# A two-block transformer on one core: the second block's indexer moved ahead of retention, its softmax heads and gated linear attention moved with it, and the head norms computed from columns

## The chip, the cores and the metric

The kernel runs on one core of a Trainium2 chip. The metric is the device time of one execution in microseconds (us). TensorE is called PE here, VectorE DVE, ScalarE ACT, GpSimd POOL and SyncE SP.

## What is computed

All values are float32, the batch is one, the sequence has 512 tokens and the model 1024 columns. A first block of two layers (mLSTM, a Fourier branch, a convolution, an MLP) is untouched. The second block has two layers, each of this form (shortened from the reference; every line is 512 rows):

```
h   = rms_norm(x, pre_norm) * (1 + scale) + shift
p   = split(h @ w_in)                       # 7764 columns
ret = retention(rope(p.ret_q), rope(p.ret_k), p.ret_v)      # 4 heads, chunks of 128
ret = rms_norm(ret) * silu(p.ret_g)         # norm per head, over its 128 columns
# indexer: for each query a score of each visible key, the 128 best are kept
score = sum_h idx_w[h] * relu(rope(p.idx_q[h]) @ rope(p.idx_k).T / 8), causal
sel   = top_k(score, 128)
dsa = softmax(rope(p.dsa_q) @ rope(p.dsa_k).T / 8, keys in sel) @ p.dsa_v   # 8 heads, 2 kv heads
dsa = dsa * silu(p.dsa_g)
log_a = log_sigmoid(p.gla_a @ gla_w_lr + gla_b_lr) / 16
gl  = rms_norm(gla(p.gla_q, p.gla_k, p.gla_v, log_a)) * silu(p.gla_g)       # norm per head
g   = sigmoid(p.merge)                      # three gates of 1024 columns
y   = (g0 * (ret @ w_br_ret) + g1 * (dsa @ w_br_dsa) + g2 * (gl @ w_br_gla)) @ w_out
x   = x + gate * rms_norm(y, post_norm)
```

## The kernel before, in words

**Layout.** Activations stay in SBUF with the columns on the partitions and the tokens along the free dimension. Weights stream from HBM in slabs of 128 x 1024 values through a ring of six. A product against `w_in_2` is made exact enough by splitting: ACT copies a slab to the rounded form `WHI` (L2051), POOL subtracts it from the slab to give `RGR` (L2440), and PE runs three rounded matmuls for each of the eight row blocks (L985 to L987). A piece "F" is 128 output columns for all tokens, 24 matmuls. A piece "T" (L1007 to L1009) gives values with the tokens on the partitions. A piece "N" (L1028) multiplies the gated result of a branch by its output weights with four unsplit matmuls, each of which shows as two records.

**One order for all engines.** `schedule()` writes one list of steps. Each engine's program walks the same list and emits its part of each step, so the order in each engine's queue is the order of the list; an instruction that waits holds all behind it on its engine. Main work is written by `products()`. Side work is laid beside it: `begin(steps, period, credit)` opens a list, and after each part of a main piece `weave(us)` adds the part's planned microseconds to the list's credit and pops one step for each `period`. An F piece has three parts and 5.6 planned us, an N piece one part and 3.5, a T task 5.8. `end()` writes what is left of a list with nothing between. `products()` ends with `flush()`, which writes the pending second halves (`post`) of the last pieces.

**PSUM.** Main pieces of the second block take the banks 0 and 1 in turn; the first matmul of a piece waits until the last reader of its bank is done. A roped piece is copied out by ACT, and its `post` (one piece later) is a matmul with a permutation into bank 7 (L1148) and three DVE instructions (L1465, L1468, L1470); bank 7 is reused by the next.

**A second-block layer before** is, in order:
1. products ret_q, ret_k (roped), ret_v (T), ret_g, nothing beside them;
2. products idx_q, idx_k, the small columns `few`, dsa_q, dsa_k, dsa_v, dsa_g; beside them retention (`ret`, four chunks of three steps) and its norms (`rSq`, `rNorm`), period 3.5;
3. products gla_q, gla_k, gla_v (T), gla_g and branch 0 (eight F for the gates, eight N); beside them three lists: `top` (the indexer's products `idx`, L1324, L2357, L1879, and the selection `top`, L1891 and L1893, for the query blocks 1 to 3), period 2.2, and `head[0]`, `head[1]` (each 4 blocks x 4 heads x 3 steps), period 2.6;
4. branch 1; beside it `gated_stages` (the decays `gDecay`, `gStart`, eight levels of `gLevel`, `gOut`, `gState`, and the norms `gSq`, `gNorm`), period 2.4, 34 steps; what is left follows at once;
5. branch 2 and the product with w_out, nothing beside them.

**The selection.** Sixteen rounds per query block, each `max` (the 8 largest, L1891) and `match_replace` (L1893, which shows as a short load of the values and the replacement). Block b has 128(b+1) keys.

**A softmax head** (block b, head t of half q) is: PE logits into bank 3+q (L1338); DVE adds the mask (L1910), takes the maximum (L1912), negates it (L1914); ACT exponential with sum (L2365); DVE reciprocal (L1916) and scaling (L1918); PE transposes (L1343); a copy by DVE for q=0 (L1922) or ACT for q=1 (L2369); PE product with the values (L1350). DVE's part up to L1918 is one step, so DVE waits in it for ACT.

**A head norm** before: ACT squares (L2342, L2417), PE multiplies 128 x 512 squares by ones (L1313, L1414), ACT takes the root over 128 x 512 (L2348, L2423), DVE inverts 128 x 512 values (L1864, L2009), multiplies the head by them (L1866, L2011) and the silu gate by that (L1868, L2013).

**The decays** (`gDecay`, twice): PE L1360, four ACT instructions (L2376 to L2382) with table loads, DVE L1935 to L1941; then `gStart`: ACT L2386, DVE, ACT L2388, DVE, ACT L2393. The gate of a branch's F piece is a sigmoid on ACT (L2246), written right after the piece. A level of `gLevel` needs two DVE products of 128 x 1024 (L1969, L1970), after which PE (L1378) and the masked copies (L1983) go.

Of the kernel before, what the change touches and what calls it, by code (L numbers as in the profile page):

```python
# [9 lines left out]
ALU = mybir.AluOpType  # L10
# [13 lines left out]
ZD = 11264  # L24
# [37 lines left out]
def constants():  # L62
# [31 lines left out]
    put("causal", np.where(i[None, :] <= i[:, None], 0.0, NEG))  # L94
# [502 lines left out]
def second_layer(o, l):  # L597
# [6 lines left out]
    def T(c0, n, dst):  # L604
        return ("T", "w_in_2", l, 0, c0, n, "v2", None, {**g, "tiles": range(4), "dst": dst})
# [88 lines left out]
def design(nc, dram):  # L694
# [135 lines left out]
    GRS = [ar(ZD + 6144, 512), ar(ZD + 6656, 512)]  # L830
# [72 lines left out]
    def tensor(e):  # L903
# [404 lines left out]

        def rNorm(l, h):
            if h >= 2:  # L1310
                e.wait_ge(*at("retA", ("sqrt", l, h - 2)))
            e.wait_ge(*at("retA", ("square", l, h)))
            e.matmul(PB[2 + h % 2][:, :], ones, RSQ[h % 2], start=True, stop=True).then_inc(*up("retP", ("norm", l, h)))  # L1313

        def idx(l, b, h):
# [3 lines left out]
            if (b, h) == (1, 0):  # L1319
                e.wait_ge(*at("evacV", ("roped", o.last["roped", l, "evacA", "DIK"])))  # L1320
                e.wait_ge(*at("retV", ("norm", l, 3)))
            else:
                e.wait_ge(*at("topA", (l, b, h - 1) if h else (l, b - 1, 3)))
            e.matmul(PB[2][:, 0:nk], DIQ[r, t, b * 128:b * 128 + 128], DIK[r, 0, 0:nk], start=True, stop=True).then_inc(*up("topP", (l, b, h)))  # L1324

        def head(l, q, b, t, i):
# [18 lines left out]
            else:  # L1345
                e.wait_ge(*at((V, A)[q], (l, b, t, "PT")))
                if t == 0 and b:
                    e.wait_ge(*at(V, (l, b - 1, "gated")))
                for kt in range(b + 1):
# [59 lines left out]

        def gNorm(l, h):  # L1410
            if h >= 2:
                e.wait_ge(*at("glaA", ("sqrt", l, h - 2)))
            e.wait_ge(*at("glaA", ("square", l, h)))
            e.matmul(PB[2 + h % 2][:, :], ones, GSQ[h % 2], start=True, stop=True).then_inc(*up("glaP", ("norm", l, h)))  # L1414

        stages = {"mm": mm, "post": post, "xsum": xsum, "rstd": rstd, "residual": residual, "mPrep": mPrep, "mA": mA, "mB": mB, "mC": mC, "mD": mD, "mO": mO,
                  "ret": ret, "rNorm": rNorm, "idx": idx, "head": head, "gDecay": gDecay, "gLevel": gLevel, "gOut": gOut, "gState": gState,
                  "gNorm": gNorm}
# [4 lines left out]
    def vector(e):  # L1423
# [436 lines left out]

        def rNorm(l, h):
            rs, g = RRS[h % 2], G2["RETG"]
            e.wait_ge(*at("retA", ("sqrt", l, h)))
            e.reciprocal(rs, rs).then_inc(*up("retV"))  # L1864
            e.wait_ge(*now("retV"))
            e.tensor_tensor(RO[:, h, :, :], RO[:, h, :, :], v4(rs), MUL).then_inc(*up("retV"))  # L1866
            e.wait_ge(*now("retV"))
            e.tensor_tensor(v4(g[:, h, :]), v4(g[:, h, :]), RO[:, h, :, :], MUL).then_inc(*up("retV", ("norm", l, h)))  # L1868
# [13 lines left out]
        def top(l, b, i):  # L1882
            nk = 128 * (b + 1)
            sl = slice(b * 128, b * 128 + 128)
            if i == 0:
                e.wait_ge(*now("topV"))
                e.tensor_tensor(SC[:, sl], SC[:, sl], cst("causal"), ADD).then_inc(*up("topV"))
            for n in range(4 * i, 4 * i + 4):
# [685 lines left out]
```

## Time and profile before

| | us |
|---|---|
| median of 3 runs (lowest, highest) | 3643.05 (3642.25, 3647.4) |
| the profiled execution: its own time | 3641.63 |
| its span | 3639.8 |
| PE busy | 3236.4 (89%) |
| DVE busy | 1446.1 (40%) |
| ACT busy | 1064.6 (29%) |
| POOL busy | 966.5 (27%) |

The span runs from the first to the last instruction of the profiled execution; its own time is measured around it. PE's share of the whole says little on one stage: the stretches of the two layers of the second block begin at about 2066 us and 2873 us in the span, and are read one by one. The granted clock stands as a fraction of full speed: 1.00 is 2.4 GHz throughout, 0.50 is 1.2 GHz throughout.

### The profile page before, as it was taken

Reading aid. Unit: us, or ns where it says so; the run is one execution under the profiler, and the core shown is the slowest. Engines: PE = TensorE matmul, PEld = TensorE weight load, DVE = VectorE, ACT = ScalarE, POOL = GpSimd, SP = SyncE. Lnnn points to the kernel's source line nnn. Section 1 sums busy time; section 2 is a strip of 40 time slices with the busy share of each in tenths; the row PEclk is TensorE's granted clock in tenths of the full one; section 3 lists DMA queues with packets and bytes.
Section 4 is the critical chain, followed back from the end, with each engine's and each line's share of the span. In section 5 each row is a group of like instructions: output and inputs, shape, how many; then the busy total and the mean of one; then the engine's idle time right before and its main releaser. Section 6 shows DMA issues by size and latency. Waiting matters only on the chain.

```text
span 3639.8 us, 40425 instructions
## 1 busy us (share of the span) xinstructions
PE 3236.4 (89%) x16416; PEld 2511.0 (69%) x16416; DVE 1446.1 (40%) x2646; ACT 1064.6 (29%) x1668; POOL 966.5 (27%) x476
## 2 busy tenths in 40 slices
PE   6989789999999889689999899797899899797898
PEld 4678668888888668577777676554657776554656
DVE  1574433422332562435111425733531326732632
ACT  2213433321222312432323223243222223234222
POOL 0121113222224112133444233121125233111134
PEclk9999877999999799789999899899899799898899
DMA  5233331211111223213222212111012112111111
GB/s 189 96 119 111 131 135 47 70 64 61 62 64 64 77 93 128 87 58 108 93 93 93 70 65 66 38 47 52 29 54 91 64 65 67 38 47 46 35 63 65
DMA packets 78505, 277.29 MB, mean 76 GB/s; under 512 B 8416, under 2 KB 10080, under 8 KB 78192
## 3 DMA queue, kind: packets, MB, share of 16 engines
q1 hardware_dynamic: 74736, 267.86, 21.6%
q10 hardware_dynamic: 3584, 6.84, 0.5%
q8 instruction: 131, 2.15, 0.2%
q14 instruction: 54, 0.44, 0.0%
HBM read 272.57 MB, written 2.10 MB: 75 GB/s over the span
## 4 chain that ended last, share of the span: by engine, by line
PE 78%; DVE 13%; ACT 5%; issue 2%; DMA 1%; POOL 1%; ACTq 0%; DVEq 0%; SPq 0%; POOLq 0%
PE pb L985 17%; PE pb L987 16%; PE pb L986 16%; PE pb L1028 5%; PE pb L1096 3%; PE pb L1378 2%; PE pb L934 2%; PE pb L1007 1%; PE pb L1009 1%; PE pb L1008 1%; DVE AR L1893 1%; DVE AR L1891 1%; PE pb L1350 1%; PE pb L1338 1%; PE pb L1054 1%
## 5 line engine op out<-in xcount | busy, mean ns | idle before, releaser
L2440 POOL TENSOR_TENSOR RGR<-RG,WHI 128x1024 fp32r<-128x1024 f32 x330 | 794.0, 2407 | 2166.4 <-ACT WHI L2051 2166.4
L2051 ACT ACTIVATE WHI<-RG 128x1024 fp32r<-128x1024 f32 x330 | 345.1, 1046 | 368.2 <-PE pb L987 282.3
L985 PE MATMUL pb<-HI,WHI 128*128 128x512 f32 (+1 forms) x880 | 389.6, 443 | 24.2 <-POOL RGR L2440 11.1
L986 PE MATMUL pb<-HI,RGR 128*128 128x512 f32 (+1 forms) x880 | 357.9, 407 | 0.0
L987 PE MATMUL pb<-LO,WHI 128*128 128x512 f32 (+1 forms) x880 | 357.8, 407 | 0.0
L985 PE MATMUL pb<-HR,WHI 128*128 128x512 f32 (+1 forms) x768 | 278.8, 363 | 16.7 <-POOL RGR L2440 10.1
L987 PE MATMUL pb<-HR,WHI 128*128 128x512 f32 (+1 forms) x768 | 277.6, 361 | 0.0
L986 PE MATMUL pb<-HR,RGR 128*128 128x512 f32 (+1 forms) x768 | 277.3, 361 | 0.0
L987 PE MATMUL pb<-HIDR,WHI 128*128 128x512 f32 (+1 forms) x768 | 274.7, 358 | 0.0
L985 PE MATMUL pb<-HIDR,WHI 128*128 128x512 f32 (+1 forms) x768 | 273.7, 356 | 1.1 <-ACT RLT L2193 0.8
L986 PE MATMUL pb<-HIDR,RGR 128*128 128x512 f32 (+1 forms) x768 | 274.1, 357 | 0.0
L985 PEld LDWEIGHTS pb<-HI,WHI 128*128 128x128 f32 (+1 forms) x880 | 171.3, 195 | 96.6 <-issue 50.0
L1028 PE MATMUL pb<-AR,RG 128*128 128x512 f32 x384 | 193.9, 658 | 15.4 <-DVE AR L2013 15.4
L987 PEld LDWEIGHTS pb<-LO,WHI 128*128 128x128 f32 (+1 forms) x880 | 170.9, 194 | 44.7
L986 PEld LDWEIGHTS pb<-HI,RGR 128*128 128x128 f32 (+1 forms) x880 | 171.5, 195 | 43.0 <-issue 8.3
L1629 DVE TENSOR_TENSOR RLT<-RLT 128x256 f32<-128x256 f32 (+1 forms) x96 | 117.7, 1226 | 206.3 <-ACT RLT L2193 206.0
L985 PE MATMUL pb<-HH,WHI 128*128 128x512 f32 (+1 forms) x464 | 173.5, 374 | 23.6 <-POOL RGR L2440 10.5
L985 PEld LDWEIGHTS pb<-HR,WHI 128*128 128x128 f32 x768 | 146.8, 191 | 47.1 <-issue 24.2
L986 PE MATMUL pb<-HH,RGR 128*128 128x512 f32 (+1 forms) x464 | 166.6, 359 | 0.0
L987 PE MATMUL pb<-HL,WHI 128*128 128x512 f32 (+1 forms) x464 | 166.5, 359 | 0.0
L987 PEld LDWEIGHTS pb<-HR,WHI 128*128 128x128 f32 x768 | 146.8, 191 | 22.9
L986 PEld LDWEIGHTS pb<-HR,RGR 128*128 128x128 f32 x768 | 147.1, 192 | 22.5
(381 smaller groups left out, 5812.1 us busy)
## 6 DMA issues: line engine op xcount, KB each, us to landing
RG<-in_W_dram SPq DMA_DIRECT2D x504, 512.0 KB, 3.3
XCX<-in_xT_dram ACTq DMA_DIRECT2D x1, 2048.0 KB, 21.3
GRID<-in_grid_dram ACTq DMA_DIRECT2D x1, 2048.0 KB, 27.2
out_dram<-XCX SPq DMA_DIRECT2D x8, 256.0 KB, 2.0
CS<-in_CST_dram ACTq DMA_DIRECT2D x1, 1027.0 KB, 4.9
XCC<-in_ctxT_dram ACTq DMA_DIRECT2D x1, 1024.0 KB, 14.9
CS<-in_CST_dram SPq DMA_DIRECT2D x1, 523.0 KB, 4.6
RG<-in_W_dram SPq DMA_DIRECT2D x2, 256.0 KB, 2.9
```

Source lines behind the costliest of these rows:

```text
L934: i = e.matmul(PB[p["banks"][0]][32 * g:32 * g + 32, 0:256], CV[:, :, 4 * h + g], wt[:, g, :], start=h == 0, stop=h == 1, tile_position=(0 ...
L985: e.matmul(out, hi[:, k, :], xh, start=k == order[0], stop=False)
L986: e.matmul(out, lo[:, k, :], xh, start=False, stop=False)
L987: i = e.matmul(out, hi[:, k, :], xl, start=False, stop=k == order[7])
L1007: e.matmul(out, xh[:, sl], hi[:, k, :], start=h == 0 and i0 % per == 0 and k == 0, stop=False)
L1008: e.matmul(out, xh[:, sl], lo[:, k, :], start=False, stop=False)
L1028: i = e.matmul(out, wt[:, k, p["j"]:p["j"] + 128], G2[p["x"]][:, k, :], start=k == 0, stop=k == 3)
L1096: m = e.matmul(sum_at(tag, c), squares_at(tag, i)[:, a:a + 128], ones[:, 0:1], start=k == 0 and c == first, stop=k == 7 and c == 5)
L1378: m = e.matmul(PB[2 + bk][:, a:a + 128], ks[r, t, sl], qs[r, t, sl], start=True, stop=True)
L1629: e.tensor_tensor(r, r, r, MUL).then_inc(*up("evacV", ("hidden", i)))
L2051: e.activation(WHI[:, u % 2, 0:n], RG[:, s % RING, 0:n], ACT.Copy).then_inc(*up("weightsA", u))
L2440: e.tensor_tensor(RGR[:, s % RING, 0:n], RG[:, s % RING, 0:n], WHI[:, u % 2, 0:n].bitcast(F32), SUB).then_inc(*up("weightsG", u))
```

## The change

- **Order.** A layer begins with idx_q, idx_k and `few`. Then ret_q, ret_k, ret_v, ret_g with `top` beside them, period 3.0; `top` goes on beside dsa_q, dsa_k, dsa_v, dsa_g, where retention and its norms are also laid, period 2.5. Selection steps now hold two rounds instead of four (24 steps instead of 12).
- **Heads.** The two lists of heads, period 2.5, lie beside gla_q, gla_k, gla_v, gla_g and the first six jobs of branch 0 (three quarters of it). Beside the last quarter lie `gDecay`, `gDecay`, `gStart` (period 4.0, credit 4.0), and the rest of `gated_stages` lies beside branch 1 (period 2.0, credit -4.0, 33 steps).
- **Norms.** The gate is multiplied by the unnormed head at once. The squares are summed by PE against one column of ones, four matmuls per head, into 16 columns of bank 3; ACT takes one root and DVE one reciprocal of 128 x 16; PE spreads the factors, four 128 x 128 matmuls per head into banks 2 to 5; DVE multiplies the gate by them from PSUM.
- **Signs.** The mask is subtracted the other way round and the minimum taken, so that the negation (L1914) goes.
- **Banks.** The T tasks of ret_v write banks 2, 3 and then 0, 1; those of gla_v banks 0, 1 and then 2, 7. The indexer's products go to bank 6 instead of 2. Some tiles move in SBUF.

```diff
 def norm_stages(x, l):
-    out = []
-    for h in range(4):
-        out += [(x + "Sq", l, h)]
-        if h:
-            out += [(x + "Norm", l, h - 1)]
-    return out + [(x + "Norm", l, 3)]
+    return [(x + "Sq", l, h) for h in range(5)] + [(x + "Root", l)] + [(x + "Norm", l, h) for h in range(4)]
...
-    jobs = [F(C_RQ, 256, "roped", "evacA", dst="RQ"), F(C_RK, 256, "roped", "evacA", dst="RK"), T(C_RV, 512, "RVT"),
-                F(C_RG, 512, "silu", "evacA", dst="RETG")]
+    jobs = [F(C_IQ, 256, "roped", "evacA", dst="DIQ"), F(((C_IK, 64), (C_IK, 64)), 128, "roped", "evacA", dst="DIK"),
+            F(((C_GA, 16), (C_IW, 4)), 20, "few", "evacA")]
...
     o.products(jobs, (0, 1), 2)
-    ret = o.begin([("ret", l, c, i) for c in range(4) for i in range(3)] + norm_stages("r", l), 3.5)
-    o.products([F(C_IQ, 256, "roped", "evacA", dst="DIQ"), F(((C_IK, 64), (C_IK, 64)), 128, "roped", "evacA", dst="DIK"),
-                F(((C_GA, 16), (C_IW, 4)), 20, "few", "evacA"), F(C_DQ, 512, "roped", "evacA", dst="DQ"),
+    top = []
+    for b in (1, 2, 3):
+        top += [("idx", l, b, h) for h in range(4)] + [("top", l, b, i) for i in range(8)]
+    top = o.begin(top, 3.0)
+    o.products([F(C_RQ, 256, "roped", "evacA", dst="RQ"), F(C_RK, 256, "roped", "evacA", dst="RK"), T(C_RV, 512, "RVT", ((2, 3), (0, 1))),
+                F(C_RG, 512, "silu", "evacA", dst="RETG")])
+    ret = o.begin([("ret", l, c, i) for c in range(4) for i in range(3)] + norm_stages("r", l), 2.5)
+    o.products([F(C_DQ, 512, "roped", "evacA", dst="DQ"),
                 F(((C_DK, 64), (C_DK, 64), (C_DK + 64, 64), (C_DK + 64, 64)), 256, "roped", "evacA", dst="DK"),
                 F(C_DV, 128, "vheads", "evacA"), F(C_DG, 512, "silu", "evacA", dst="DSAG")])
     o.end(ret)
-    top = []
-    for b in (1, 2, 3):
-        top += [("idx", l, b, h) for h in range(4)] + [("top", l, b, i) for i in range(4)]
-    head = [[("head", l, q, b, t, i) for b in range(4) for t in range(4) for i in range(3)] for q in range(2)]
-    sides = [o.begin(top, 2.2), o.begin(head[0], 2.6, 1.3), o.begin(head[1], 2.6)]
-    o.products([F(C_GQ, 256, "gq", "evacA"), F(C_GK, 256, "cp", None, dst="GK"), T(C_GV, 512, "GVT"), F(C_GG, 512, "silu", "evacA", dst="GLAG")])
+    o.end(top)
+    heads = [o.begin([("head", l, q, b, t, i) for b in range(4) for t in range(4) for i in range(3)], 2.5, 1.25 * q) for q in range(2)]
+    o.on_bank[2] = ("retV", ("norm", l, 3))
+    o.on_bank[7] = ("evacA", ("turned", o.last["vheads", l, "evacA", None]))
+    o.products([F(C_GQ, 256, "gq", "evacA"), F(C_GK, 256, "cp", None, dst="GK"), T(C_GV, 512, "GVT", ((0, 1), (2, 7))),
+                F(C_GG, 512, "silu", "evacA", dst="GLAG")])
+    gated = gated_stages(l)
...
+        if br == 0:
+            o.products(jobs[0:6])
+            o.end(*heads)
+            start = o.begin(gated[0:3], 4.0, 4.0)
+            o.products(jobs[6:8])
+            o.end(start)
+            gated = o.begin(gated[3:], 2.0, -4.0)
+            continue
         o.products(jobs)
-        if br == 0:
-            o.end(*sides)
-            sides = [o.begin(gated_stages(l), 2.4)]
         if br == 1:
-            o.end(*sides)
+            o.end(gated)
...
+        def head_sums(h, squares):
+            for c in range(4):
+                m = e.matmul(PB[3][:, 384 + 4 * h + c:385 + 4 * h + c], squares[:, c * 128:c * 128 + 128], ones[:, 0:1], start=h == 0 and c == 0,
+                             stop=h == 3 and c == 3)
+            return m
+        def head_factors(h, roots):
+            for c in range(4):
+                m = e.matmul(PB[2 + h][:, c * 128:c * 128 + 128], roots[:, 4 * h + c:4 * h + c + 1].to_broadcast([128, 128]), ident, start=c == 0,
+                             stop=c == 3)
+            return m
...
-            e.reciprocal(rs, rs).then_inc(*up("retV"))
-            e.tensor_tensor(RO[:, h, :, :], RO[:, h, :, :], v4(rs), MUL).then_inc(*up("retV"))
-            e.tensor_tensor(v4(g[:, h, :]), v4(g[:, h, :]), RO[:, h, :, :], MUL).then_inc(*up("retV", ("norm", l, h)))
+            g = G2["RETG"][:, h, :]
+            e.tensor_tensor(g, g, PB[2 + h][:, :], MUL).then_inc(*up("retV", ("norm", l, h)))
...
-                e.tensor_tensor(L, PB[3 + q][:, 0:nk], MAS[b][:, 0:nk], ADD).then_inc(*up(V))
+                e.tensor_tensor(L, MAS[b][:, 0:nk], PB[3 + q][:, 0:nk], SUB).then_inc(*up(V))
-                e.tensor_reduce(mx, L, AX, MAX).then_inc(*up(V))
-                e.tensor_scalar(mx, mx, -1.0, None, MUL).then_inc(*up(V, (l, b, t, "max")))
+                e.tensor_reduce(mx, L, AX, MIN).then_inc(*up(V, (l, b, t, "max")))
```

## Rows read from the trace of the kernel before

**Rows 1.** The page's fourth part: the chain that ended last, by engine

```profile
PE 78%; DVE 13%; ACT 5%; issue 2%; DMA 1%; POOL 1%; ACTq 0%; DVEq 0%; SPq 0%; POOLq 0%
```

**Rows 2.** Stretches of layer one: length, PE, PEld, DVE, ACT, POOL busy; clock, DMA

```profile
2103.00:2246.00 143.00, 138.62 (x617) 101.84 (x617) 54.88 (x64) 43.31 (x60) 45.81 (x20) 1.00 0.21 68
2246.00:2319.00 73.00, 52.50 (x245) 36.69 (x243) 49.27 (x154) 18.04 (x43) 14.15 (x6) 0.84 0.15 49
2319.00:2380.00 61.00, 49.19 (x228) 35.35 (x228) 43.98 (x103) 19.00 (x33) 11.87 (x5) 0.85 0.11 35
2380.00:2520.00 140.00, 125.96 (x490) 76.39 (x490) 45.44 (x101) 50.45 (x75) 23.64 (x10) 0.96 0.15 49
2520.00:2645.00 125.00, 98.55 (x438) 70.64 (x437) 66.02 (x81) 39.28 (x41) 19.90 (x9) 0.84 0.10 34
2645.00:2708.00 63.00, 54.14 (x223) 35.25 (x222) 27.65 (x29) 19.48 (x30) 17.42 (x9) 0.95 0.18 59
```

**Rows 3.** Waits of PE in 2246:2520: total us, times, longest

```profile
PE pb L1343 <- DVE AR L1918: 29.1, 13, 6.9
PE pb L1007 <- DVE AR L1647: 14.8, 1, 14.8
```

**Rows 4.** Waits of PE in 2520:2720

```profile
PE pb L1378 <- ACT AR L2393: 15.9, 1, 15.9
PE pb L1378 <- DVE AR L1970: 10.6, 6, 3.1
PE pb L1028 <- DVE AR L2013: 7.7, 1, 7.7
```

**Rows 5.** DVE by line in 2246:2380: busy, mean ns, idle before

```profile
L1891 DVE MAX8 AR<-AR 128x8 f32<-128x256 f32 (+2 forms) x48 | 26.9, 561 | 1.5
L1893 DVE MATCH_REPLACE8 AR<-AR 128x256 f32<-128x256 f32 (+2 forms) x48 | 26.0, 542 | 0.0
L1879 DVE SCALAR_TENSOR_TENSOR AR<-AR 128x256 f32<-128x256 f32 (+2 forms) x9 | 8.2, 908 | 16.2 <-ACT AR L2357 16.1
```

**Rows 6.** DVE by line and shape in 2110:2720

```profile
L1864 DVE RECIPROCAL AR<-AR 128x512 f32<-128x512 f32 x4 | 13.4, 3351 | 9.1 <-ACT AR L2348 9.1
...
L1891 DVE MAX8 AR<-AR 128x8 f32<-128x512 f32 x16 | 11.1, 694 | 0.5
L1893 DVE MATCH_REPLACE8 AR<-AR 128x512 f32<-128x512 f32 x16 | 10.8, 676 | 0.0
...
L1465 DVE TENSOR_TENSOR AR<-AR,TAB 128x512 f32<-128x512 f32 x9 | 8.3, 927 | 0.0
...
L1866 DVE TENSOR_TENSOR AR<-AR 128x512 f32<-128x512 f32 x4 | 5.8, 1451 | 0.1
...
L1868 DVE TENSOR_TENSOR AR<-AR 128x512 f32<-128x512 f32 x4 | 4.8, 1210 | 0.1
```

**Rows 7.** ACT in order of time around the decays: start, us, what, idle before

```profile
2525.37 0.69 ACT L2376 ACTIVATE AR<-pb,VC 128x512 f32<-128x512 f32 x1 [10.58 <-PE pb L1360]
...
2538.24 0.60 ACT L2246 ACTIVATE AR<-pb 128x512 f32<-128x512 f32 x1
...
2550.84 0.60 ACT L2246 ACTIVATE AR<-pb 128x512 f32<-128x512 f32 x1
```

**Rows 8.** PE: a wait in ret_v; then the first and last matmul of an F piece

```profile
2089.82 0.36 PE L1007 MATMUL pb<-WHI,HI 128*128 128x256 f32 x1 [2.20 <-DVE AR L1647]
...
2527.91 0.50 PE L985 MATMUL pb<-HI,WHI 128*128 128x512 f32 x1
...
2533.39 0.40 PE L987 MATMUL pb<-LO,WHI 128*128 128x512 f32 x1
```

**Rows 9.** PE: sums against a column of ones, and spread factors, four matmuls each

```profile
2815.74 0.95 PE L1130 MATMUL pb<-CS,AR 128*128 128x1 f32 x8
...
2820.08 2.07 PE L1104 MATMUL pb<-CS,RSS 128*128 128x128 f32 x8 [1.64 <-DVE RSS L1496]
```

**Rows 10.** PE by shape in 2090:2820: retention's 16 matmuls of 128 columns

```profile
L1294 PE MATMUL pb<-AR 128*128 128x128 f32 x32 | 6.6, 303 | 0.0
```

More of the change, by code:

```diff
@@ L1307, in ret, with rSq @@
                 m.then_inc(*up("retP", (l, c, "KV")))
+        def head_sums(h, squares):
[8 more added lines that the diff above has]
+            return m
+        def rSq(l, h):
+            if h:
+                e.wait_ge(*at("retA", ("square", l, h - 1)))
+                head_sums(h - 1, RSQ[(h - 1) % 2]).then_inc(*up("retP", ("sums", l, h - 1)))
         def rNorm(l, h):
[L1310 to L1313, printed above, removed]
+            e.wait_ge(*at("retV", ("root", l)))
+            head_factors(h, RRS).then_inc(*up("retP", ("norm", l, h)))
         def idx(l, b, h):
@@ L1348, in head @@
                     e.wait_ge(*at(V, (l, b - 1, "gated")))
+                elif t == 0 and q:
+                    e.wait_ge(*at("topA", (l, 3, 3)))
                 for kt in range(b + 1):
@@ L1408, in gState, with gSq @@
             m.then_inc(*up("glaP", (l, c, "KV")))
+        def gSq(l, h):
+            if h:
+                e.wait_ge(*at("glaA", ("square", l, h - 1)))
+                head_sums(h - 1, GSQ[(h - 1) % 2]).then_inc(*up("glaP", ("sums", l, h - 1)))
         def gNorm(l, h):
[L1411 to L1414, printed above, removed]
+            e.wait_ge(*at("glaV", ("root", l)))
+            head_factors(h, GRS).then_inc(*up("glaP", ("norm", l, h)))
         stages = {"mm": mm, "post": post, "xsum": xsum, "rstd": rstd, "residual": residual, "mPrep": mPrep, "mA": mA, "mB": mB, "mC": mC, "mD": mD, "mO": mO,
-                  "ret": ret, "rNorm": rNorm, "idx": idx, "head": head, "gDecay": gDecay, "gLevel": gLevel, "gOut": gOut, "gState": gState,
-                  "gNorm": gNorm}
+                  "ret": ret, "rSq": rSq, "rNorm": rNorm, "idx": idx, "head": head, "gDecay": gDecay, "gLevel": gLevel, "gOut": gOut, "gState": gState,
+                  "gSq": gSq, "gNorm": gNorm}
         for what in o.steps:
@@ L1859, in ret, with rSq, rRoot @@
                               PB[4][:, 0:256].rearrange("p (t i) -> p t i", t=2)).then_inc(*up("retV", (l, c, "out")))
-        def rNorm(l, h):
-            rs, g = RRS[h % 2], G2["RETG"]
-            e.wait_ge(*at("retA", ("sqrt", l, h)))
-            e.reciprocal(rs, rs).then_inc(*up("retV"))
-            e.wait_ge(*now("retV"))
-            e.tensor_tensor(RO[:, h, :, :], RO[:, h, :, :], v4(rs), MUL).then_inc(*up("retV"))
-            e.wait_ge(*now("retV"))
-            e.tensor_tensor(v4(g[:, h, :]), v4(g[:, h, :]), RO[:, h, :, :], MUL).then_inc(*up("retV", ("norm", l, h)))
+        def rSq(l, h):
+            if h < 4:
+                g = v4(G2["RETG"][:, h, :])
+                if h == 0:
+                    e.wait_ge(*at("evacA", o.last["silu", l, "evacA", "RETG"]))
+                    e.wait_ge(*at("retA", (l, 3, "out")))
+                    e.wait_ge(*at("retV", (l, 3, "out")))
+                e.tensor_tensor(g, g, RO[:, h, :, :], MUL).then_inc(*up("retV", ("gated", l, h)))
+        def rRoot(l):
+            e.wait_ge(*at("retA", ("root", l)))
+            e.reciprocal(RRS, RRS).then_inc(*up("retV", ("root", l)))
+        def rNorm(l, h):
+            g = G2["RETG"][:, h, :]
+            e.wait_ge(*at("retV", ("gated", l, h)))
+            e.wait_ge(*at("retP", ("norm", l, h)))
+            e.tensor_tensor(g, g, PB[2 + h][:, :], MUL).then_inc(*up("retV", ("norm", l, h)))
         def idx(l, b, h):
@@ L1886, in top @@
                 e.wait_ge(*now("topV"))
-                e.tensor_tensor(SC[:, sl], SC[:, sl], cst("causal"), ADD).then_inc(*up("topV"))
-            for n in range(4 * i, 4 * i + 4):
+                e.tensor_tensor(SC[:, sl], SC[:, sl], cst("causal"), SUB).then_inc(*up("topV"))
+            for n in range(2 * i, 2 * i + 2):
                 src = SC if n == 0 else WK
@@ L2352, in idx @@
             e.wait_ge(*at("topP", (l, b, h)))
-            if (b, h) == (1, 0):
-                e.wait_ge(*at("retV", ("norm", l, 3)))
-            else:
+            if (b, h) != (1, 0):
                 e.wait_ge(*at("topV", (l, b, h - 1, "sum") if h else (l, b - 1, 3, "sum")))
-            e.activation(RLU[:, 0:nk], PB[2][:, 0:nk], ACT.Relu).then_inc(*up("topA", (l, b, h)))
+            e.activation(RLU[:, 0:nk], PB[6][:, 0:nk], ACT.Relu).then_inc(*up("topA", (l, b, h)))
         def head(l, q, b, t, i):
```

84 lines of the change are left out of this document (46 added, 38 removed).

## The prediction, made blind

> **What bounds the kernel now.** I read the chain first, then PE's waits, then stretches, then DVE and ACT inside them. The chain gives PE 78% and DVE 13% [rows 1]: the end is set by PE, which at some places waits for DVE. Those places are in the second block. In layer one PE is idle 4.4 us of 143 while retention runs (length less busy), 20.5 + 11.8 = 32.3 us of 134 where selection and the first heads run, 14.0 of 140 in the later heads, 26.5 of 125 in the decays and levels, 8.9 of 63 in the GLA outputs and norms: 86.1 us [rows 2]. Layer two repeats this within a few us, so every term counts twice.
>
> The reader is to see two more things in these rows. Where PE hardly waits the granted clock is 1.00; where it waits much it is 0.84 or 0.85, and in the late heads, whose 14 us of waits are short ones, still 0.96 [rows 2]. And DVE is busy 93 of 134 us in the first heads but only 45 of 140 after them: the difference is the selection, 26.9 + 26.0 + 8.2 = 61.1 us [rows 5]. DVE takes its steps in order, so heads and PSUM evacuations stand behind rounds of selection. One piece of gla_v waited 14.8 us for its bank that way [rows 3].
>
> **The change part by part**, for one layer, in us of PE's time (minus is gain).
>
> *Selection leaves the heads.* The first heads keep only their own chain, as the late ones have it. The 14.8 us of gla_v go, as DVE has no backlog and each T pair now has banks of its own. Of 32.3 us I leave 2, since blocks 0 and 1 have short rows: -30. Bounds: if the early heads waited at the late heads' rate, 14.0 / 140 x 134 = 13 stay (-19); at best all goes (-32).
>
> *Late heads.* Same products, same N pieces of 3.5 planned us that let two head steps meet without main work between; the negation goes, and the period falls from 2.6 to 2.5, which takes back about as much: -1, bounds -5 to +3.
>
> *Selection goes to retention's side.* 36 steps of 3.0 planned us are 108, over 67.9 + 61.6 = 129.5 planned us: all fit. Beside ret_q to ret_g DVE has little else. The tight place is block 3: its eight selection steps fall 19 to 40 us into the second group of products. DVE must do 16 x (0.694 + 0.676) = 22 us and the loads between [rows 6], four roped posts at 3 x 0.93 = 11 at most [rows 6], and about 9 of retention and gates: 42. PE has 21 of main work and some 13 of retention and ropes beside it: 34. Each retention step and each rope waits for DVE's step before it, so PE can't run ahead: 8 us of wait, 2 more for steps that meet a two-round step of 2.7 us: +10. Bounds: 3 (the excess absorbed by the light steps behind) and 48 (rival C). The same region had 4.4 us of waits, mostly behind the norm's root and DVE's 3.35 us reciprocals; of these I take 3.4 away. Net +6.6.
>
> *The first products.* ret_v's wait of 2.2 us for its bank [rows 8] goes, with the banks split. But the new first group ends with `few`, and the flush behind it makes PE wait for its copy (0.6, as the 0.60 of a bank [rows 7]) and for DVE's rope of idx_k (2 x 0.93 [rows 6]), with no piece between: +2.3. Together 0, bounds -2 to +2.
>
> *Norms by columns.* DVE loses 13.4 + 5.8 + 4.8 = 24.0 us per norm [rows 6] and gets four products into the gate (1.21 each), four from PSUM and one tiny reciprocal: about 8. At the end of GLA the reciprocals were what PE waited for: 7.7 [rows 4]. The new norm ends inside branch 1 and two F pieces pass before its reader: of 8.9 us [rows 2], -7.7. PE pays: 16 sums per norm. Four take 0.95 at full clock [rows 9]: 4.0. And 16 spreads, between 2.07 / 4 / 2 = 0.26 (that row ran at half clock) [rows 9] and 6.6 / 16 = 0.41 [rows 10], together 4.2 to 6.6, against four ones-products of about 0.87, 3.5, that go. So +4.7 to +7.1 per norm; I take 6, and +12 for two.
>
> The Trainium skill ("SBUF — State Buffer", section "Who interferes with whom") says that a DVE instruction with two SBUF inputs and a GpSimd instruction that reads SBUF exclude each other for their whole length. This case fits: L1866 and L1868 have two SBUF inputs and average 1.45 and 1.21 us [rows 6], over a one-input instruction's 0.69. It speaks for the multiplication from PSUM, and against laying 12 index sums, which have two SBUF inputs, beside products whose slabs POOL splits all the time; their 0.91 average [rows 5] has that in it only in part.
>
> *Decays beside branch 0.* This is where I differ most from what the order suggests. The wait of 15.9 us [rows 4] is the time of a serial chain ACT - DVE - ACT. From its first ACT instruction at 2525.37, the sigmoid of the F piece then in work leaves its bank at 2538.84 (+13.5), and that of the next one at 2551.44 (+26.1), because both stand behind decay steps in ACT's queue [rows 7]. The new order has the same shape: `gDecay` after the first part of the seventh job, `gDecay` at its end, ahead of that piece's sigmoid, `gStart` inside the next piece, ahead of its sigmoid. With a piece of 5.5 to 5.7 us [rows 8], PE starts the quarter at 0, the chain begins at 3.3, both F pieces are done at 13.3. The N piece behind needs the bank of the first: free at 16.8, a wait of 3.5. It takes 3.6; the second N needs the other bank: free at 29.4, a wait of 9.0. So 12.5 instead of 15.9: -3.4. Bounds: 0 if the sigmoids come through (-15.9), and 16.
>
> *Levels.* Per level PE offers 4 x 1.03 of its own and two steps' worth of main work, which falls from 4.8 to 4.0; DVE's two products, powers and masked copies don't change. The six waits of together 10.6 [rows 4] grow by about 0.4 each: +2.5, bounds 0 to +6. No steps are left over at branch 1's end any more (33 x 2.0 + 4 = 70 of 72.8 planned).
>
> *Clock.* (1 - clock) x length is 20.8 us in the early heads, 5.6 in the late, 20.0 in the decays and levels, 3.2 in the norms [rows 2]. Work loses this only while PE is busy, 0.76, 0.90, 0.79 and 0.86 of it: 15.8 + 5.0 + 15.8 + 2.8 = 39. The early heads give most back (-13), the norm its part and what the first pieces behind it lost (-4); the new waits beside retention take 4. So -13, bounds 0 to -25.
>
> The Trainium skill ("TensorE: Matmul & The Clock Gate", section "HAM oscillation — how this bites in real kernels") has PE fall back to the slow clock after idle gaps and prices throttled time at one half of it, as I do. The trace agrees only for the long waits: ten short ones left 0.96. If each new wait threw the clock back as the page's oscillating kernel shows, the 13 us would be none.
>
> Sum for a layer: -30 - 1 + 6.6 + 0 - 7.7 + 12 - 3.4 + 2.5 - 13 = -34.0; twice, -68. The profiled execution (3641.63, span 3639.8 and 1.8 around it) lies 1.4 under the median of 3643.05; from it the sum gives 3573.6, from the median 3575. I predict **3574**.
>
> **Rivals.**
>
> A, *the heads' waits are the price of their own chain*: early heads keep 13 us rather than 2, and the clock gives back nothing. For it: L1343's 29.1 us in 13 waits [rows 3], of which 14.0 us remain once selection is over [rows 2]. Against: blocks 0 and 1 have a quarter and a half of the last block's keys. Per layer -34 + 11 + 13 = -10: 3623. The clock rule of the page leads here too, by its half (-34 + 13 = -21: 3601).
>
> B, *the stalls go almost wholly*: the decays' sigmoids come through and leave 2 us (10.5 less), retention meets 4 (6 less), the norm costs 9 (3 less), the clock returns 25 (12 more). Per layer -34 - 31.5 = -65.5: 3512. For it: 1.00 in the stretch with retention now, though dense; against: the queue order above.
>
> C, *slower: DVE becomes the bound beside retention*. Twelve retention steps and four ropes each wait for a full selection step, 2 x 1.37 + 0.3 = 3.0: 48 us instead of 10, and the 60 us of main products beside them run at half clock, up to +30. Per layer -34 + 38 + 30 = +34: 3711. It decides from 34 us more wait and slow clock than I count. Against: rounds of blocks 1 and 2 are shorter, and DVE idles 88 of 143 us in that stretch now [rows 2].
>
> D, *no change*: the waits are the same ones under other names: new ones beside retention and in branch 0's end, and 12 us of added PE work, equal what goes; 3643. For it only the decays' part, which does so.
>
> **How the numbers follow.** Forecast 0.50, A 0.15, B 0.22, C 0.08, D 0.05. The range runs from 3505, just past B, to 3630, past A, and leaves C, D and a little of B's tail out. The likeliest case's own bounds: the terms at their near ends, some 17 us a layer either way, 3540 to 3608. About 0.2% (7 us) is what a measurement can tell from no change. Faster by more than that: forecast, A, B, less a little: 0.86. Within: D, 0.05. Slower: C and what is unforeseen, 0.09.
>
> **What would show it.** In the trace after: no wait of L1007 on DVE above 1 us; the early heads at clock near 1.00; waits of retention's lines or L1148 on the selection (L1891 to L1893) of 5 to 15 us a layer; a wait of an N piece (L1028) for ACT's sigmoid near the end of branch 0 of about 9 us; L1378's waits on DVE of 10 to 15; no wait on the last norm; DVE busy about 70 us less in all (16 per norm, 5 per layer for the negations). Wrong would be: more than 20 us of waits beside retention (C), more than 10 in the early heads (A), or under 4 at branch 0's end (B).

## The result and the profile after

The changed kernel took 3577.48 us in the median (3576.69 to 3578.79, four runs) against 3642.65 for the kernel before (3642.07 to 3647.4) on the same chip: ratio 0.9819, 95% interval 0.9802 to 0.9836. The forecast was 3574.0. The profiled execution has a span of 3574.9 us, 64.9 less than before.

From the first rope product of the second block's layer one to that of layer two it is 808.7 before and 773.4 after (-35.3), from there to the end 771.4 and 739.9 (-31.5), and the first block is 1.9 longer: -64.9.

From the page after, busy time by engine and then the chain that ended last, by engine:

```profile
PE 3236.3 (91%) x16640; PEld 2526.4 (71%) x16640; DVE 1374.9 (38%) x2570; ACT 1060.7 (30%) x1660; POOL 962.5 (27%) x476
...
PE 81%; DVE 10%; ACT 5%; issue 2%; DMA 1%; POOL 1%; ACTq 0%; DVEq 0%; SPq 0%; POOLq 0%
```

DVE went from 13% to 10% of the chain [rows 1] and has 71 us less work in all (forecast: about 70). Next, layer one of the second block in stretches, with columns as in [rows 2]. They are: indexer and first products; retention; early heads; late heads; decays; levels; GLA outputs and norm; the rest up to the next layer's first products.

```profile
2068.00:2165.00 97.00, 92.85 (x462) 69.83 (x464) 50.83 (x120) 23.83 (x34) 33.46 (x14) 0.97 0.21 71
2165.00:2271.00 106.00, 99.86 (x459) 73.87 (x457) 62.61 (x112) 26.62 (x39) 24.67 (x11) 0.94 0.16 53
2271.00:2361.00 90.00, 84.42 (x457) 64.23 (x457) 28.34 (x79) 30.67 (x62) 25.90 (x11) 0.98 0.19 62
2361.00:2487.00 126.00, 106.72 (x427) 65.92 (x425) 40.44 (x82) 47.66 (x71) 18.84 (x8) 0.92 0.14 46
2487.00:2519.00 32.00, 21.77 (x58) 11.84 (x57) 10.81 (x19) 20.40 (x22) 4.69 (x2) 0.84 0.10 33
2519.00:2609.00 90.00, 79.75 (x394) 59.18 (x393) 51.65 (x63) 21.50 (x21) 14.60 (x8) 0.91 0.13 41
2609.00:2665.00 56.00, 54.76 (x267) 38.80 (x266) 13.24 (x24) 19.96 (x28) 14.83 (x8) 1.00 0.14 47
...
2665.00:2842.00 177.00, 164.25 (x667) 123.09 (x665) 40.83 (x58) 47.02 (x67) 76.40 (x45) 0.90 0.24 81
```

To balance a whole layer, two stretches of the kernel before are needed that [rows 2] leaves out, ahead of and behind its six:

```profile
2066.00:2103.00 37.00, 33.76 (x220) 30.78 (x220) 7.72 (x10) 5.28 (x7) 10.74 (x5) 0.89 0.18 58
2708.00:2876.00 168.00, 154.71 (x613) 114.22 (x612) 40.08 (x58) 44.65 (x63) 72.21 (x42) 0.88 0.23 79
```

A stretch's first number less PE's busy time is PE's idle time. Over the layer it was 86.1 + 3.2 + 13.3 = 102.6 us before (810 us long) and is 69.6 after (774 us long): 33.0 less. The busy time fell by 3.0, from 707.4 to 704.4. So the layer's gain of 36 is nearly all waits. The 3.0 is what the clock gave back, less the work that the norms added. Layer two says the same: of its 31.4 us, 30.8 are idle time (107.1 to 76.3) and 0.6 busy time.

Waits of PE after, in the stretches 2165:2271, 2271:2361, 2361:2487 and 2487:2780, one fence (columns as in [rows 3]):

```profile
PE pb L1319 <- ACT AR L2391: 3.3, 1, 3.3
PE pb L1301 <- DVE AR L1867: 1.6, 1, 1.6
PE pb L1291 <- DVE AR L1886: 1.2, 1, 1.2
...
PE pb L1366 <- DVE AR L1954: 5.0, 5, 2.6
...
PE pb L1366 <- DVE AR L1954: 16.2, 9, 4.4
...
PE pb L1403 <- DVE AR L2006: 10.2, 6, 3.1
PE pb L1035 <- ACT AR L2293: 10.2, 2, 7.2
PE pb L1419 <- DVE AR L2039: 1.2, 1, 1.2
```

L1366 is the heads' transposes (L1343 before [rows 3]), L1403 the levels (L1378 [rows 4]), L1035 the N pieces (L1028), L1319 the new sums, L1291 and L1301 retention. The 14.8 of gla_v [rows 3], the 15.9 of the decays and the 7.7 of the last norm [rows 4] are gone. New are 10.2 at N pieces and 3.3 at the sums. Of the heads' waits before, 17.1 in 6 fell in 2246:2380 and 12.0 in 7 behind it.

### The profile page after: what moved, and what is told of

Its sections match the earlier page's. It is cut to its first block, busy times and chain, and to the rows that moved or that the text cites. A ratio compares the mean times of both kernels' runs of the same rounds, so it can differ in the third digit from the quotient of the medians.

```text
span 3574.9 us, 40795 instructions
## 1 busy us (share of the span) xinstructions
PE 3236.3 (91%) x16640; PEld 2526.4 (71%) x16640; DVE 1374.9 (38%) x2570; ACT 1060.7 (30%) x1660; POOL 962.5 (27%) x476
## 4 chain that ended last, share of the span: by engine, by line
PE 81%; DVE 10%; ACT 5%; issue 2%; DMA 1%; POOL 1%; ACTq 0%; DVEq 0%; SPq 0%; POOLq 0%
PE pb L992 18%; PE pb L994 17%; PE pb L993 17%; PE pb L1035 4%; PE pb L1103 3%; PE pb L1403 2%; PE pb L941 2%; PE pb L1014 2%; PE pb L1015 1%; PE pb L1016 1%; PE pb L1375 1%; PE pb L1061 1%; PE pb L1361 1%; PE pb L1111 1%; DVE AR L1624 1%
## 5 line engine op out<-in xcount | busy, mean ns | idle before, releaser
L1035 PE MATMUL pb<-AR,RG 128*128 128x512 f32 x384 | 189.7, 644 | 20.6 <-ACT AR L2293 20.6
```

Of the source, the lines that this page charges most:

```text
L1035: i = e.matmul(out, wt[:, k, p["j"]:p["j"] + 128], G2[p["x"]][:, k, :], start=k == 0, stop=k == 3)
```

## Experiments

A layer's length below is the 808.7 or 773.4 of above, taken the same way in the profiled execution of each kernel. In the versions of the changed kernel PE has the same instructions, so where a layer's busy time differs, they ran at another pace, in the main at another granted clock; only the idle time is waits. Both layers of every version, in us:

| kernel | layer one: length, idle, busy | layer two: length, idle, busy |
|---|---|---|
| before | 808.7, 101.6, 707.1 | 771.4, 107.1, 664.3 |
| before, norms alone | 797.7, 90.8, 706.9 | 765.0, 95.2, 669.8 |
| before, selection cut | 776.6, 78.5, 698.1 | 740.1, 84.7, 655.4 |
| changed | 773.4, 69.0, 704.4 | 739.9, 76.3, 663.7 |
| changed, again | 773.4, 69.0, 704.5 | 739.9, 76.3, 663.7 |
| changed, selection cut | 759.9, 62.9, 696.9 | 730.8, 68.9, 661.9 |
| `gStart` later | 764.7, 65.6, 699.1 | 735.1, 71.3, 663.9 |
| second `gDecay` later too | 776.6, 65.9, 710.7 | 737.8, 72.3, 665.5 |
| N pieces in halves | 776.0, 66.1, 709.9 | 739.2, 73.5, 665.7 |
| `gStart` later and halves | 767.8, 63.5, 704.3 | 734.9, 69.1, 665.8 |
| heads half a cycle apart | 759.0, 55.2, 703.9 | 728.3, 60.9, 667.5 |
| heads apart, `gStart` later | 759.6, 51.5, 708.1 | 724.2, 57.8, 666.4 |
| selection's period 2.6 | 776.9, 68.6, 708.3 | 744.4, 76.6, 667.8 |

**Norms alone.** The kernel before with only the new norms: `norm_stages`, sums, root and factors as in the change, order and heads untouched.

```diff
-    out = []
-    for h in range(4):
-        out += [(x + "Sq", l, h)]
-        if h:
-            out += [(x + "Norm", l, h - 1)]
-    return out + [(x + "Norm", l, 3)]
+    return [(x + "Sq", l, h) for h in range(5)] + [(x + "Root", l)] + [(x + "Norm", l, h) for h in range(4)]
```

> The kernel before with the column norms alone (order, banks, signs of before). Theory: DVE loses 16 us a norm; of PE's waits about 3.4 + 5 us beside retention and the first heads go, and the 7.7 us before branch 2; the clock gives 4 back; PE pays 8.6 us a layer (the 8.5 us of sums, 8.3 of spreads against 8.2 of ones-products read in the changed kernel). About -11 us a layer: 3620. Rival: the added PE work is all that shows, since other waits take the freed DVE time: +17, 3660. Second rival: the norms carry most of the change: 3590 or less.

Measured 3627.98 us (ratio to the kernel before 0.9951, 95% interval 0.9935 to 0.9968; the other runs are given in the same way); the layer is 797.7, 11.0 shorter. Its waits in the heads and decays:

```profile
PE pb L1355 <- DVE AR L1943: 28.5, 13, 6.9
PE pb L1002 <- DVE AR L1662: 14.8, 1, 14.8
...
PE pb L1390 <- ACT AR L2428: 15.9, 1, 15.9
PE pb L1390 <- DVE AR L1995: 10.5, 6, 3.0
```

They are those of [rows 3, 4] but for the 7.7 of the last norm, which is missing. Also gone are 3.4 us of waits for POOL's split (5.6 to 2.2 in the layer), which stood behind the old norm beside retention. The 5 us that the expectation took from the first heads did not go. With 8.6 us of work added, the layer's busy time stayed (707.1, 706.9), so its clock gave that much back; in layer two it gave back only 3.1. By length, the norms account for 11 of 35 us in layer one and 6.4 of 31.4 in layer two, and what is left, some 24 and 25, goes with the order, signs and banks. That split holds if the two add; the order alone was not run.

**Selection cut short, in the kernel before and in the changed one.** 4 of each block's 16 rounds are kept, 12 left out.

```diff
-            for n in range(4 * i, 4 * i + 4):
+            for n in range(i, i + 1):
```

> The kernel before with 4 of the 16 selection rounds in each query block (the other 12 are left out, so more keys stay masked out than should). Theory (DVE's backlog of selection is what the early heads wait for): the 14.8 us of gla_v and most of the 26.5 us of head waits before 2380 go, early heads keep about 5 us, clock there above 0.95; about -37 us a layer: 3570. Rival A (the heads' own chain is the price): 13 us or more of waits stay there beside a clock near 0.88; about -20 a layer: 3603.

```diff
-            for n in range(2 * i, 2 * i + 2):
+            for n in range(i // 2, i // 2 + 1 - i % 2):
```

> The changed kernel with 4 of the 16 selection rounds of each block kept and 12 left out (the same cut as in the kernel before, which there gave 3580.7 us, 62 to 65 us less). It tells how much the selection still costs in the new order. Theory (in the new order VectorE does the rounds beside products that don't wait for it): only the 5 to 8 us per layer of waits beside retention go, with 1 to 3 of clock, 3577 - 16 = about 3561 us. Rival (the selection still slows the layer through VectorE's queue and the shared memory everywhere): 30 to 45 us go, 3532 to 3547 us.

Measured 3580.7 (0.9825, 0.981 to 0.984) and 3555.7 (0.976, 0.9745 to 0.9774). In the kernel before the cut takes 62 to 65 us, in the changed one 22; by layer one 32.1 (to 776.6) and 13.5 (to 759.9). First the waits that the kernel before keeps with the cut, then those of the changed one, in the heads:

```profile
PE pb L1343 <- DVE AR L1918: 16.0, 12, 3.4
PE pb L1007 <- DVE AR L1647: 4.8, 1, 4.8
```

```profile
PE pb L1366 <- DVE AR L1954: 21.2, 14, 4.4
```

In the old place the selection cost 13.1 us of the heads' 29.1 and 10.0 of gla_v's 14.8. All of the 13.1 lie in the early heads (17.1 to 4.0); the late ones keep their 12.0. In the new place the heads' waits are the same with and without the rounds (5.0 + 16.2 above, 21.2 here), so nothing of them is selection. What the rounds still cost stands beside retention: with the cut the view of PE's waits lists none there, and the 6.1 us above are gone; the other 7.5 us of layer one (1.8 in layer two) are busy time, so clock. That is the move of the selection shown from both sides. The kernel before without the rounds is about as fast as the changed kernel with them.

**The decays' steps against the sigmoids.** Two orders of the same steps beside the last quarter of branch 0. `rest` is a step that does nothing.

```diff
-            start = o.begin(gated[0:3], 4.0, 4.0)
+            start = o.begin(gated[0:2] + [("rest",)] + gated[2:3], 4.0, 4.0)
```

> The changed kernel with gStart one part later, after the second sigmoid of branch 0's last quarter in ACT's queue. Theory (PE's wait of 7.2 us is for a sigmoid that stands behind gStart's three exponentials): that wait goes, the first of 3.0 stays, the levels start in time; -7 us of wait and -2 of slow clock a layer: 3560. Rival: the serial chain is the bound, and the same us come back as a wait of the first level: 3575 to 3578.

Measured 3563.85 (0.9777, 0.9763 to 0.9792), 13.6 us under the changed kernel. Its layers are 8.7 and 4.8 shorter; of these, 3.4 and 5.0 are waits, and 5.3 us of layer one are busy time. ACT in order of time, in the changed kernel (start, duration, instruction, idle before):

```profile
2500.40 0.60 ACT L2293 ACTIVATE AR<-pb 128x512 f32<-128x512 f32 x1
...
2503.25 1.06 ACT L2431 ACTIVATE AR<-AR 128x1024 f32<-128x1024 f32 x1
2506.96 1.06 ACT L2433 ACTIVATE AR<-AR 128x1024 f32<-128x1024 f32 x1 [2.65 <-DVE AR L1994]
2510.64 1.06 ACT L2438 ACTIVATE AR<-AR 128x1024 f32<-128x1024 f32 x1 [2.62 <-DVE AR L1985]
...
2513.01 0.60 ACT L2293 ACTIVATE AR<-pb 128x512 f32<-128x512 f32 x1
```

and in this one:

```profile
2500.62 0.60 ACT L2293 ACTIVATE AR<-pb 128x512 f32<-128x512 f32 x1
...
2502.06 0.59 ACT L2293 ACTIVATE AR<-pb 128x512 f32<-128x512 f32 x1
```

The second sigmoid (L2293) stood behind three exponentials (L2431 to L2438) and two waits for DVE, and comes 11 us sooner when it stands ahead of them. The N pieces' waits fall from 10.2 to the first one's 3.0. A new one of 3.5 appears, a bank that DVE's gateY holds, as gateY now stands behind DVE's part of `gStart`. So the N pieces' wait is a matter of place in ACT's queue, as the prediction had it. The total lands near the 3560 expected partly by luck: net waits fell by 8 us over both layers, not 14, and layer one's clock gave 5 more that its waits don't explain.

```diff
-            start = o.begin(gated[0:3], 4.0, 4.0)
+            start = o.begin([gated[0], ("rest",), gated[1], gated[2]], 4.0, 4.0)
```

> The changed kernel with the second gDecay after the first sigmoid and gStart after the second. Theory: both N pieces' waits (3.0 and 7.2 us a layer) shrink to under 2, one more table load each way on ACT; -8 us of wait and -3 of clock a layer: 3556. Rival: the chain is stretched by the sigmoids and ends about 5 us too late for the first level: 3565. Second rival (chain is the bound anyway): 3577.

Measured 3581.53 (0.9826, 0.9812 to 0.9841): a miss of 25 us. The waits for the sigmoids fell nearly as expected, from 10.2 to 2.2, but one of 4.8 for a bank that gateY holds (L1689) came in, which neither the theory nor its rivals had:

```profile
PE pb L992 <- DVE AR L1689: 4.8, 1, 4.8
PE pb L1035 <- ACT AR L2293: 2.2, 1, 2.2
```

7.0 against the changed kernel's 10.2, yet layer one is 3.2 longer. The layer in the changed kernel, with `gStart` later, and here (columns as in [rows 2]):

```profile
2061.54:2834.95 773.41, 704.38 (x3179) 506.75 (x3178) 298.16 (x556) 237.66 (x343) 213.25 (x104) 0.93 0.18 59
2061.67:2826.38 764.71, 699.10 (x3180) 504.09 (x3179) 298.62 (x556) 237.65 (x343) 213.27 (x104) 0.94 0.18 60
2069.28:2845.87 776.59, 710.69 (x3179) 511.31 (x3178) 297.88 (x556) 239.03 (x344) 213.26 (x104) 0.92 0.18 59
```

The idle time is 3.1 less here and the busy time of the same instructions 6.3 more, at a lower clock. Part of it lies behind the levels: in a stretch of 62 us PE was busy 60.76 us in both, but at a granted clock of 1.00 in the changed kernel and 0.94 here, about 3.6 us. Layer two, with the same edit, is 2.1 shorter, and the second block starts 7.7 later though nothing ahead of it differs. So this run tells little of the edit, and why its clock was lower is open.

**The changed kernel again, unaltered.**

> The changed kernel unaltered, on the same chip as the two others, to have its profile a second time: how far do two executions of the same instructions stand apart, and where. Expected: 3577 to 3580 us, each layer of the second block within 2 us of 774 us; the rival, that a kernel's lengths move by 5 us or more from load to load, would put the differences of the small experiments in doubt.

Measured 3581.68 (0.9828, 0.9813 to 0.9843), 4.2 us above the first time (the kernel before, run beside it, was 1.9 above its first time). Both layers are as long as the first time, and its second block starts at 2066.0 instead of 2061.5: all of the difference in span (3579.4 against 3574.9) arose in the first block. The four executions of this kernel lie between 3578.26 and 3585.01, and those of each of the two kernels with the heads moved, below, stand 9 us apart. So a difference in the total that is smaller than that says little of an edit; the idle time of the layer edited says more, and its length does where the busy time is the same.

**Heads: two guesses at the late waits.** First, N pieces handed out in halves with steps between:

```diff
-        return {"ada": 1.5, "N": 3.5, "G": 2.0}.get(p["kind"], 1.0)
+        return {"ada": 1.5, "N": 1.75, "G": 2.0}.get(p["kind"], 1.0)
...
-                    self.run(p, [(0, 1, 2, 3)], 3.5)
+                    self.run(p, [(0, 1), (2, 3)], 3.5)
```

> The changed kernel with one edit: the eight matmuls of an N piece are emitted as two parts of four with a step of each side queue between them, so that the two heads' steps no longer come back to back after 3.5 us of branch product. In the changed kernel the heads' transposes wait 19.3 us per layer beside branch 0, the longest 4.4 us, at places where both heads' logits stand directly behind each other and VectorE does both chains one after the other. Theory (steps bunched by the long piece): these waits go from 19.3 to about 10 per layer and the clock comes back a little, 3577 - 2 x 9 = about 3560 us. Rival (the waits are the length of one chain of logits, minimum, exponential and transpose, however the steps are spread): they stay at 17 to 20 per layer, 3574 to 3580 us.

> Both edits together on the changed kernel: the decays' second part one step later, behind the second sigmoid in ScalarE's queue (by itself 3563.9 us), and N pieces in two parts. If the two waits are separate (the sigmoid's 7.2 us near the end of branch 0, the heads' 19.3 us beside its middle), the gains add: 3564 - 17 = about 3547 us. Rival (the heads' waits are one chain long and don't move): 3562 to 3568 us.

Measured 3580.53 (0.9825, 0.9811 to 0.984) and 3567.44 (0.9795, 0.9779 to 0.9812); layers 776.0 and 767.8, 2.6 and 3.1 longer than without the halves, though their idle time is 2 to 3 us less: the busy time is 5.5 and 5.2 more. The transposes' wait is 20.9 in 14 in both, against 21.2 in 14 of the changed kernel, the longest still 4.4. The bunching by N pieces, which the prediction also named, is not the cause.

The trace of the changed kernel shows another one. DVE in order of time around the wait of 4.42 us, with both heads' logits just done:

```profile
2449.14 0.69 DVE L1948 TENSOR_TENSOR AR<-AR,pb 128x512 f32<-128x512 f32 x1 [9.04 <-PE pb L1361]
2449.86 0.69 DVE L1950 TENSOR_REDUCE AR<-AR 128x1 f32<-128x512 f32 x1
2451.43 0.17 DVE L1952 RECIPROCAL AR<-AR 128x1 f32<-128x1 f32 x1 [0.88 <-ACT AR L2410]
2451.63 0.49 DVE L1954 TENSOR_SCALAR AR<-AR 128x512 f32<-128x512 f32 x1
2452.03 0.68 DVE L1948 TENSOR_TENSOR AR<-AR,pb 128x512 f32<-128x512 f32 x1
2452.74 0.69 DVE L1950 TENSOR_REDUCE AR<-AR 128x1 f32<-128x512 f32 x1
2454.31 0.16 DVE L1952 RECIPROCAL AR<-AR 128x1 f32<-128x1 f32 x1 [0.88 <-ACT AR L2410]
2454.51 0.48 DVE L1954 TENSOR_SCALAR AR<-AR 128x512 f32<-128x512 f32 x1
```

DVE stands 0.88 us at the first reciprocal while ACT does the exponential, with the second head's L1948 ready behind it; one head's chain is 2.9 us and the other's begins after it. Each list's three steps take 7.5 planned us, and the lists are 1.25 apart. So, half of 7.5 apart:

```diff
-... for i in range(3)], 2.5, 1.25 * q) for q in range(2)]
+... for i in range(3)], 2.5, 3.75 * q) for q in range(2)]
```

> The changed kernel with one number changed: the second head group's queue of steps begins 3.75 us of product ahead of the first's instead of 1.25, half of the 7.5 us that a tile's three steps take. In the changed kernel VectorE stands in its own queue between a head's minimum and its reciprocal while ScalarE does the exponential, so the chain of one head takes 2.7 to 2.9 us and the other's begins behind it; where both heads' logits come together (2447.98) the first transpose waits 4.4 us. Theory (the two chains collide): half a period apart they don't, and the heads' waits (21.2 us in 14 per layer beside branch 0) fall to 6 to 10, so 3577 - 2 x 14 = about 3550 us. Rival (each chain is longer than the 2.5 us of product between a head's own steps, whatever the other does): the waits stay above 16 us per layer and the time above 3568 us.

> The same together with the decays' second part one step later (by itself 3563.9 us). Theory: the two gains add, about 3538 to 3545 us. Rival (as above): 3558 to 3566 us.

Measured 3558.4 (0.9764, 0.9748 to 0.9781) and 3549.29 (0.9736, 0.9722 to 0.9751). The profiled executions are not like their medians: that of the first is its fastest (3549.64; the other three 3558.25 to 3558.77), that of the second its slowest (3551.97). The waits in the heads and the stretch of the late heads, with one number changed:

```profile
PE pb L1366 <- DVE AR L1954: 6.8, 10, 1.8
PE pb L1014 <- DVE AR L1681: 2.5, 1, 2.5
...
2361.00:2487.00 126.00, 118.78 (x484) 72.46 (x482) 44.71 (x91) 59.99 (x86) 21.29 (x9) 1.00 0.16 51
```

21.2 in 14 became 6.8 in 10, none above 1.8, and the clock of the stretch is 1.00 instead of 0.92. The layer is 14.4 shorter (759.0), 13.9 of it idle time: 14.4 of the transposes' waits went, a T piece's wait grew by 2.0, and smaller ones fell. The busy time is only 0.5 less, so what the late heads' clock gave back was nearly lost elsewhere in the layer. Layer two has the same waits (6.8 in 10) and is 11.6 shorter. The collision of the two chains is shown to be the cause of two thirds of the heads' waits.

With both edits the median is 9 us below the one edit's, but the profiled execution's span is 2.4 longer: 6.0 more in the first block, 0.6 more in layer one and 4.1 less in layer two. The idle time fell in both layers, by 3.7 and 3.1, as the N pieces' waits fell; in layer one the busy time rose by 4.2. Two stretches of 41 us in the levels and behind them, where both kernels are at the same instructions within 1.2 us, first without, then with the later `gStart`:

```profile
2555.00:2596.00 41.00, 38.33 (x217) 28.96 (x216) 29.23 (x34) 11.39 (x11) 8.97 (x5) 0.99 0.12 39
2596.00:2637.00 41.00, 39.76 (x202) 28.65 (x201) 10.33 (x19) 15.61 (x24) 8.46 (x5) 1.00 0.12 41
```

```profile
2555.00:2596.00 41.00, 38.82 (x209) 28.99 (x208) 28.43 (x34) 11.39 (x11) 7.32 (x4) 0.93 0.12 39
2596.00:2637.00 41.00, 39.76 (x181) 27.43 (x180) 10.61 (x20) 13.91 (x21) 9.29 (x5) 0.92 0.12 39
```

The idle time is the same within 0.5 us (39.76 of 41 us busy in the second stretch of both), and yet the clock is 0.92 against 1.00: about 5.5 us that the waits don't explain. At 3549.29 this is the fastest version run, 28 us under the changed kernel's first median and 32 under its second, the latter on the same chip.

**A shorter period for the selection.**

```diff
-    top = o.begin(top, 3.0)
+    top = o.begin(top, 2.6)
```

> The changed kernel with one number changed: the indexer's and the selection's steps are handed out every 2.6 us of product instead of every 3.0, so the last block's rounds end before the densest part of retention. Theory (VectorE's backlog of selection rounds beside retention is what TensorE waits for there): the waits of retention's and the norm's lines, 7.9 us per layer, fall to about 3, and the time to about 3577 - 2 x 6 = 3565 us. Rival (a round of the last block needs about 1.46 us of VectorE, two of them 2.9 us, more than 2.6, so the queue falls behind earlier and the rotated query's pieces wait instead): waits in the first products of the layer rise by 5 or more per layer, 3577 to 3590 us.

Measured 3584.3 (0.9836, 0.9822 to 0.9851); the layer is 776.9, 3.5 longer. Beside retention:

```profile
PE pb L1301 <- DVE AR L1867: 5.5, 3, 2.8
```

With 0.3 at L1291, 5.8 instead of 6.1: the wait at the sums went and retention's grew by the same. The theory fell in its size; the rival's waits in the first products didn't come either. The idle time of both layers is that of the changed kernel within 0.5 us, and their busy time 3.9 and 4.1 more: what this run lost, it lost in PE's pace, for a reason that is open.

## Why the prediction was right

The mechanism was the one forecast, PE's waits for DVE's queue. The two sides of its step list came out like this, in us of a layer, idle time from the windows:

| step | predicted | measured | from |
|---|---|---|---|
| early heads | -30 | -26.7 | 32.3 to 5.6 |
| late heads | -1 | +5.3 | 14.0 to 19.3 |
| first products and retention | +6.6 | +2.7 | 7.6 to 10.3 |
| last norm's wait | -7.7 | -7.7 | 8.9 to 1.2 |
| decays and levels | -0.9 | -6.0 | 26.5 to 20.5 |
| the rest of the layer | 0 | -0.5 | 13.3 to 12.8 |
| norms' work on PE | +12 | +8.6 | rows below |
| clock | -13 | -11.6 | busy -3.0, less +8.6 |
| sum | -34.0 | -35.9 | the same layer by its marks: -35.3 |

The waits sum to -33 in both columns; single steps missed by 3 to 6 us, in both directions. That the total came within 4 us owes something to that, and to the clock: in the experiments, layers whose idle time agrees within 0.5 us differed by 4 us of busy time.

**Early heads**: 5.6 us are left instead of 2, under A's 13. Their clock is 0.98, as forecast. A was wrong, as the cut selection shows: in the old order, too, only 16 of 29 us of the heads' waits were their own, and the short rows of the early blocks wait least (5.0 in 5, against 16.2 in 9 later). What the prediction offers for A compares unlike things: 29.1 are L1343's waits, but the 14.0 are all of PE's idle time in the late stretch, of which L1343 had 12.0.

**Late heads** failed in direction: -1 was forecast, +5.3 came. The prediction took them as unchanged work with bunching by N pieces. They were two chains in one DVE queue, at an offset of a sixth of their cycle, and putting them half a cycle apart took two thirds. Why they cost 5 more than in the old order, where the lists also stood half a step apart, no run separates.

**Retention**: the place and the releasers are right (L1291, L1301 for DVE), but the waits are 6.1 us where 10 were forecast. With the rounds cut they go. (A wait of 1.8 at an F piece behind ret_v stays with the cut, so it is not the selection's.) C's 48 was far off. The largest, 3.3 at the sums, comes by a way the prediction didn't name: ACT's square stands behind an ACT instruction that waits for DVE. The norm's root was not to be seen in any wait.

**Norms' work**: sums and spreads, both norms of a layer, and below them the ones-products of the kernel before that went:

```profile
L1319 PE MATMUL pb<-CS,AR 128*128 128x1 f32 x64 | 8.5, 254 | 3.3 <-ACT AR L2391 3.3
L1326 PE MATMUL pb<-CS,AR 128*128 128x128 f32 x64 | 8.3, 275 | 0.0
```

```profile
L1313 PE MATMUL pb<-AR,CS 128*128 128x512 f32 x8 | 4.1, 590 | 0.0
L1414 PE MATMUL pb<-AR,CS 128*128 128x512 f32 x8 | 4.1, 611 | 0.5 <-ACT AR L2417 0.5
```

8.5 + 8.3 - 8.2 = 8.6, where 12 were taken: the sums are about right (4.3 a norm against 4.0; by the row cited, four times 0.95, it would have been 3.8), the spreads are at the low end of their bounds (4.2), and four ones-products took 4.1, not the 3.5 that the prediction has from 0.87 each, a figure that no row shows.

**Decays**: the two N waits are 3.0 and 7.2, forecast 3.5 and 9.0, and both orders of the experiment move them as ACT's queue says. **Levels**: 10.2 instead of 13; less main work beside a step did not lengthen their six waits (10.6 before).

**Clock**: the size is near, in part by luck. In layer two the same reckoning gives -9.2 (busy -0.6, less 8.6). The late heads ran at 1.00 with 7.2 us idle and at 0.92 with 19.3; but a stretch with 1.2 of 41 us idle had 0.92 in one kernel and 1.00 in another. The Trainium skill ("TensorE: Matmul & The Clock Gate", section "HAM oscillation — how this bites in real kernels") has the clock fall after idle gaps. The first pair agrees; the second shows that what a stretch gets can't be told from its own waits.

## What to carry to other kernels

When two identical chains share an in-order engine with a wait inside each, set them half a cycle apart: one constant was worth about 20 us here (19 against the changed kernel's first median, 23 against its second), as much as a third of the whole change. Before moving a step for an engine's sake, read what stands behind it in every queue it enters; a sigmoid behind three exponentials made PE wait 7 us a layer. And compare small edits by PE's idle and busy time, apart, in the layer they touch, with a second profile of the unaltered kernel beside them.

## What was not expected of the hardware

- A DVE instruction with two inputs in SBUF took 2.94 us (L1498, 128x512, at 2228.78) where others of its line took 0.69, with a slab's split of 2.40 us on POOL from 2228.76 on; the mean of six beside retention was 1.28. Its neighbour with an input in PSUM (L1496) stayed at 0.69.
- Four matmuls of 128 x 1 cost as much as four of 128 x 128: 254 and 275 ns each, 8.5 and 8.3 us busy for the same number. The column form saves no time on PE, only on DVE.
- The first block, untouched by any edit, took 2059.8 to 2069.3 us from version to version, with PE busy 1865.3 us in the one and 1871.8 in the other, and differed by 4.5 us between two loads of one kernel.
